# Weight slabs of a fused recurrent block, in halves through a ring of four

## What is computed

```python
h = rms_norm(x, norm_g)
xa, ga, q, f_pre, i_in, gb, gm = split(h @ w_in)          # w_in: 1024 x 8192
ya = rg_lru(causal_conv4(xa)) * silu(ga)                  # gated linear recurrence
o  = hgrn2_chunked(silu(q), 1 - f, i_in, log(f))          # 8 heads, state 128 x 128
yb = rms_norm(o) * silu(gb)
g_a, g_b = split(sigmoid(gm + b_merge))
x = x + (g_a * (ya @ proj_a) + g_b * (yb @ proj_b)) @ w_out
return rms_norm(x, final_norm_g)
```

## Time and profile before

| | us |
|---|---|
| median of the timed runs (2) | 1841.28 |
| lowest, highest | 1828.49, 1854.06 |
| the profiled execution | 1826.28 |
| its span, slowest core (core 1) | 1824.7 |
| spans of the 8 cores | 1814.4 to 1824.7 |

### The profile page before, as it was taken

The page is one execution under the profiler, slowest core; times in us unless marked ns, Lnnn a source line. Parts: engine busy times, 40 slices in busy tenths (PEclk is TensorE's granted clock), DMA queues, the critical chain, the costliest instruction groups (busy, mean ns, idle before and its releaser), DMA issues.

```text
span 1824.7 us, 24273 instructions; the slowest of 8 cores (1814.4 to 1824.7 us)
## 1 busy us (share of the span) xinstructions
PE 1497.1 (82%) x7552; PEld 706.6 (39%) x7552; DVE 1077.5 (59%) x1764; ACT 988.4 (54%) x2007; POOL 102.7 (6%) x118
## 2 busy tenths in 40 slices
PE   1786769998698977989689985989869997899866
PEld 0332244343443434434443434434344344443342
DVE  0543465575664676656655756656667467566664
ACT  3262472657537563574826666275744757256571
POOL 0000010000100001000000001000010000100010
PEclk9898879999799998999889997999979998899978
DMA  9999936632135412354035431353213631243302
GB/s 197 197 193 180 184 92 185 223 145 95 47 138 189 170 57 93 137 187 149 37 139 172 152 139 47 109 214 139 93 56 130 231 139 47 98 179 139 139 1 92
DMA packets 33404, 243.96 MB, mean 134 GB/s; under 512 B 2048, under 2 KB 2176, under 8 KB 22016
## 3 DMA queue, kind: packets, MB, share of 16 engines
q0 software_dynamic: 22816, 185.08, 33.5%
q1 hardware_dynamic: 10464, 57.33, 9.2%
HBM read 226.15 MB, written 39.85 MB: 146 GB/s over the span
## 4 chain that ended last, share of the span: by engine, by line
PE 63%; ACT 14%; DMA 9%; issue 8%; DVE 5%; DVEq 0%; ACTq 0%; POOL 0%; POOLq 0%; SPq 0%
PE PS L394 47%; PE PS L405 9%; DMA WS<-w_in 8%; ACT SQJ L655 2%; ACT R L545 2%; DVE R L500 2%; PE PS L680 2%; ACT Q L582 1%; DVE ATT L624 1%; ACT Q L580 1%; PE PS L602 1%; ACT Q L585 1%; PE PS L649 1%; DMA wbf<-WS 1%; ACT Q L487 1%
## 5 line engine op out<-in xcount | busy, mean ns | idle before, releaser
L394 PE MATMUL PS<-HT,WS 128*128 128x512 bf16 x3584 | 801.7, 386 | 70.3 <-DMA WS<-w_in 40.6
L394 PEld LDWEIGHTS PS<-HT,WS 128*128 128x128 bf16 x3584 | 352.7, 99 | 514.6 <-issue 113.9
L548 DVE TENSOR_TENSOR_SCAN R<-ONES,R 128x512 f32<-128x512 f32 x64 | 75.4, 1210 | 142.3 <-ACT R L545 142.3
L463 DVE SCALAR_TENSOR_TENSOR R<-R,PAR 128x512 f32<-128x512 f32 x192 | 144.3, 751 | 20.4 <-DVE R L463 0.5
L443 ACT ACTIVATE HT<-PS,PAR 128x512 bf16<-128x512 bf16 x64 | 37.9, 704 | 207.6 <-PE PS L441 207.6
L500 DVE SCALAR_TENSOR_TENSOR R<-R 128x512 f32<-128x512 f32 x64 | 39.9, 692 | 182.4 <-ACT R L497 182.1
L394 PE MATMUL PS<-R,WS 128*128 128x512 bf16 x512 | 128.3, 418 | 12.9 <-DVE R L683 12.9
L394 PE MATMUL PS<-Q,WS 128*128 128x512 bf16 x512 | 115.2, 384 | 22.6 <-DVE Q L553 13.0
L405 PE MATMUL PS<-WS,HT 128*128 128x512 bf16 x512 | 117.6, 389 | 17.2 <-DVE R L504 16.6
L649 PE MATMUL PS<-R 128*128 128x128 bf16 x256 | 66.2, 266 | 64.4 <-DVE ATT L624 62.4
L405 PE MATMUL PS<-WS,Q 128*128 128x512 bf16 x512 | 112.8, 379 | 0.0
(11 more groups left out here) (106 smaller groups left out, 2077.1 us busy)
## 6 DMA issues: line engine op xcount, KB each, us to landing
WS<-wbf POOLq DMA_DIRECT2D x77, 2048.0 KB, 8.1
wbf<-WS SPq DMA_DIRECT2D x11, 2048.0 KB, 13.7
XT<-x SPq DMA_DIRECT2D x8, 2048.0 KB, 13.8
WS<-w_in POOLq DMA_DIRECT2D x8, 2048.0 KB, 31.0
y<-XT SPq DMA_DIRECT2D x8, 2048.0 KB, 13.2
WS<-proj_a POOLq DMA_DIRECT2D x1, 2048.0 KB, 23.9
WS<-proj_b POOLq DMA_DIRECT2D x1, 2048.0 KB, 24.8
WS<-w_out POOLq DMA_DIRECT2D x1, 2048.0 KB, 15.4
```

The lines of the kernel that those rows point to most:

```text
L394: P.emit("pe", lambda e, W=W, ps=ps, k=k, m=m: e.matmul(ps[:, :], W[:, k, m * 128:(m + 1) * 128], src(k), start=(k == 0), stop=(k == 7)), ...
L463: P.emit("dve", lambda e, k=k: e.scalar_tensor_tensor(XC.ap(m), XA.ap(m, k, k + TT), par(P_CW + 8 * k + m), XC.ap(m), ALU.mult, ALU.add), ...
L548: P.emit("dve", lambda e: e.tensor_tensor_scan(BB.ap(hd), ONES[:, 0:1].to_broadcast([128, TT]), SS.ap(hd), 0.0, ALU.mult, ALU.add), reads= ...
```

## The change

Each slab is cut into two halves of 512 output columns, h = 0 and 1. `WS` becomes four buffers of 128 x 8 x 512 (the same SBUF in all), each with its own buffer record and its own load and store semaphores. `wbf` has 22 entries of 8 KB in each partition. `next_w(name, h)` hands out one half and issues loads until those of the three following halves (`PREF = NWS - 1`) are issued. In tile 0 a load reads runs of 512 float32 columns (2 KB) and writes runs of 1 KB; each load has its store. `proj_fm` takes a new half at m = 0 and m = 4. `proj_tm` now has the half outside and the row groups j inside, where before j was outside.

```diff
@@ -209,7 +209,7 @@
     dram["fng"] = nc.dram_tensor("fng", [128, D], F32, kind="ExternalInput").ap()
     dram["consts"] = nc.dram_tensor("consts", [128, 256], F32, kind="ExternalInput").ap()
     dram["y"] = nc.dram_tensor("y", [NB * SEQ, D], F32, kind="ExternalOutput").ap()
-    dram["wbf"] = nc.dram_tensor("wbf", [11, 128, 8 * D], BF16, kind="Internal").ap()
+    dram["wbf"] = nc.dram_tensor("wbf", [22, 128, 8 * 512], BF16, kind="Internal").ap()
     dbg = None
     if debug is not None:
         dbg = nc.dram_tensor("dbg", list(debug), F32, kind="ExternalOutput").ap()
@@ -249,7 +249,8 @@
         ONB = sb("ONB", [128, D], BF16)
         WX = sb("WXb", [128, 8, 128], BF16)
         WA = sb("WAb", [128, 8, 128], BF16)
-        WS = [sb("WS%d" % i, [128, 8, D], BF16) for i in range(2)]
+        NWS = 4
+        WS = [sb("WS%d" % i, [128, 8, 512], BF16) for i in range(NWS)]
         b_XT = [[Buf("XT%d_%d" % (i, j)) for j in range(4)] for i in range(2)]
         b_HT = [Buf("HT%d" % c) for c in range(NCH)]
         b_SQJ, b_PAR, b_DP, b_FNG = Buf("SQJ"), Buf("PAR"), Buf("DP"), Buf("FNG")
@@ -262,7 +263,7 @@
         b_ATT4 = [Buf("ATT4_%d" % i) for i in range(2)]
         b_ONB = Buf("ONB")
         b_WX, b_WA = Buf("WX"), Buf("WA")
-        b_WS = [Buf("WS0"), Buf("WS1")]
+        b_WS = [Buf("WS%d" % i) for i in range(4)]
 
         XW = 516
         R1 = Region(nc, es, "R1", 8 * XW * 4, gran=XW * 4)
@@ -315,7 +316,7 @@
         s_ld = [sem("ld_x0"), sem("ld_x1")]
         s_c = [sem("ld_c%d" % i) for i in range(5)]
         s_st = [sem("st_y0"), sem("st_y1")]
-        s_w = [sem("ld_w0"), sem("ld_w1")]
+        s_w = [sem("ld_w%d" % i) for i in range(4)]
         out_ops = []
 
         P.emit("sp", lambda e: e.dma_start(out=PAR[:, :], in_=dram["params"]), writes=[b_PAR], dma_sem=s_c[0])
@@ -352,20 +353,21 @@
             WORDER = ["xa", "ga", "gma", "pa", "f", "q", "gb", "i"]
         else:
             WORDER = ["xa", "ga", "gma", "i", "gb", "q", "f", "pa", "gmb", "pb", "wo"]
+        NHC = 2 * len(WORDER)
+        total_w = NB * NT * NHC
         wstate = {"n": 0, "issued": 0}
-        total_w = NB * NT * len(WORDER)
-
-        b_WBF = [Buf("WBF%d" % i) for i in range(len(WORDER))]
-        s_wst = [sem("st_w0"), sem("st_w1")]
+        b_WBF = [Buf("WBF%d" % i) for i in range(NHC)]
+        s_wst = [sem("st_w%d" % i) for i in range(NWS)]
+        PREF = NWS - 1
 
         def issue_w(idx):
             if idx >= total_w:
                 return
-            k = idx % len(WORDER)
-            name = WORDER[k]
-            s = idx % 2
-            if idx < len(WORDER):
-                src = WSRC[name].rearrange("(k p) n -> p k n", p=128)
+            k = idx % NHC
+            name, h = WORDER[k // 2], k % 2
+            s = idx % NWS
+            if idx < NHC:
+                src = WSRC[name][:, h * 512:(h + 1) * 512].rearrange("(k p) n -> p k n", p=128)
                 P.emit("pool", lambda e, s=s, src=src: e.dma_start(out=WS[s][:, :, :], in_=src),
                        writes=[b_WS[s]], dma_sem=s_w[s], name="ldw_" + name)
                 P.emit("sp", lambda e, s=s, k=k: e.dma_start(out=dram["wbf"][k], in_=WS[s][:, :, :].rearrange("p k n -> p (k n)")),
@@ -374,35 +376,37 @@
                 P.emit("pool", lambda e, s=s, k=k: e.dma_start(out=WS[s][:, :, :].rearrange("p k n -> p (k n)"), in_=dram["wbf"][k]),
                        reads=[b_WBF[k]], writes=[b_WS[s]], dma_sem=s_w[s], name="ldwb_" + name)
 
-        def next_w(name):
+        def next_w(name, h):
             idx = wstate["n"]
-            assert WORDER[idx % len(WORDER)] == name, (name, WORDER[idx % len(WORDER)])
-            if idx == 0:
-                issue_w(0)
-            issue_w(idx + 1)
+            assert WORDER[(idx % NHC) // 2] == name and idx % 2 == h, (name, h, idx)
+            while wstate["issued"] <= min(idx + PREF, total_w - 1):
+                issue_w(wstate["issued"])
+                wstate["issued"] += 1
             wstate["n"] = idx + 1
-            return WS[idx % 2], b_WS[idx % 2]
+            return WS[idx % NWS], b_WS[idx % NWS]
 
         def proj_fm(wname, src, src_bufs, consume, before=None):
-            W, bW = next_w(wname)
             for m in range(8):
+                if m % 4 == 0:
+                    W, bW = next_w(wname, m // 4)
                 if before is not None:
                     before(m)
                 P.lab = wname
                 ps, bps = next_ps()
+                mm = m % 4
                 for k in range(8):
-                    P.emit("pe", lambda e, W=W, ps=ps, k=k, m=m: e.matmul(ps[:, :], W[:, k, m * 128:(m + 1) * 128], src(k), start=(k == 0), stop=(k == 7)),
+                    P.emit("pe", lambda e, W=W, ps=ps, k=k, mm=mm: e.matmul(ps[:, :], W[:, k, mm * 128:(mm + 1) * 128], src(k), start=(k == 0), stop=(k == 7)),
                            reads=[bW] + src_bufs(k), writes=[bps])
                 consume(m, ps, bps)
 
         def proj_tm(wname, src, src_bufs, consume):
-            W, bW = next_w(wname)
-            P.lab = wname
-            for j in range(4):
-                for half in range(2):
+            for half in range(2):
+                W, bW = next_w(wname, half)
+                P.lab = wname
+                for j in range(4):
                     ps, bps = next_ps()
                     for k in range(8):
-                        P.emit("pe", lambda e, W=W, ps=ps, k=k, j=j, half=half: e.matmul(ps[:, :], src(k, j), W[:, k, half * 512:(half + 1) * 512], start=(k == 0), stop=(k == 7)),
+                        P.emit("pe", lambda e, W=W, ps=ps, k=k, j=j: e.matmul(ps[:, :], src(k, j), W[:, k, :], start=(k == 0), stop=(k == 7)),
                                reads=[bW] + src_bufs(k), writes=[bps])
                     consume(j, half, ps, bps)
 
```

## The result

The changed kernel takes 1849.02 us (median of 11 runs) beside 1830.69 us for the kernel before (median of 10). The ratio is 1.0096, 95% interval 1.0076 to 1.0117: about 18 us slower, inside the 2% that was called no change, and on the other side of the 5 us of gain that were forecast. The median before that the prediction started from, 1841.28, came from two runs; over more it is 1830.69, near the profiled execution.

A forecast was written before the change was run, and what follows sets the result against it. Tile 0's full DMA stretch before gmb was taken as the bound; -5 - 6 + 6 + 0 = -5 us gave 1821 from the profiled execution, 1836 from the median. Forecast 1832, between them, called no change; range 1806 to 1866.

The forecast's parts named there:

- What bounds the kernel: Full DMA stretch before gmb of tile 0, a row of weight loads; later tiles keep 215.1 us and can't gain.
- Half a slab less: Ahead of gmb in tile 0: its first half needs 8.5 slabs loaded, not 9; gain 5 us, bounds 0 and 7.3.
- tails: Tile 0 loads: the queue empties before each landing, three halves in flight fill it; gain 6 us, bounds 0 and 8.
- Shorter rows: Tile 0 loads: 2 KB runs double the packets, with 23 ns each independent of size; +6 us, bounds 0 and +132.
- The Trainium skill on run length: Tile 0 loads: line rate from 512 B up, so the short-run term would be 0 and the time 6 us lower.
- Twice as many transfers: All weight transfers: some 2.5 us fixed per transfer lie beside other transfers; cost 0, without that cover +43 us.
- Rival C: Tile 0 transfers: the per-transfer part isn't hidden, half of 43 us shows; +10 us, 1842 us, chance 0.08.
- POOL, order of the loops, the added wait: More POOL reload issues, proj_tm's exchanged loops and PE's wait in mid-slab: each cost 0; bounds 42 us for POOL, 2 for order.
- The base: Time before the change: profiled execution 1826.28 us, median of two timed runs 1841.28; forecast 1832 lay between 1821 and 1836.
- B: Tile 0 stream gets quicker through finer mixing, 208 GB/s for 191; 23 us faster, 1814 us, chance 0.16.
- D: The ring does nothing, transfer time in tile 0 is moved, not saved; 0 to -2 us, 1836 us, chance 0.12.
- A: Tile 0 loads: a 2 KB run costs 0.65 of a 4 KB one (149 ns); +29 us, 1861 us, chance 0.22.

The follow-up runs named there:

- The run with neighbouring runs: Changed kernel, but in tile 0 eight loads take both halves of a slab row by row, as neighbouring 2 KB runs; 0.995 of the kernel before, 1819.09 us.
- the control with two slabs and eight loads: Kernel before, with each slab loaded in tile 0 by eight DMAs of 128 whole rows, runs of 4 KB; 0.9959 of the kernel before.
- The run with two ahead: Changed kernel with two halves issued ahead instead of three (PREF = NWS - 2), nothing else changed; 1.01 of the kernel before.
- the run cut by rows: Kernel before with its two slabs, each slab cut by k into two DMAs for load, store and reload, runs of 4 KB; 0.9969, 1822.29 us.

## Why the prediction was wrong, point by point

- *What bounds the kernel.* Right. The period of the later tiles moved by 0.3 us, PE never waits for a reload, and the difference is there before `gmb` of tile 0. Putting off bytes moved tile 0: 29 us in `pb` for eight stores (38 were expected for `gmb`), and 8 us in the whole for one x tile (5 to 6 expected).
- *Half a slab less, and tails: -5 and -6.* Neither term was measured by itself. In the changed kernel the first half of `gmb` came 13 us later than before and not 7 sooner, under the dearer loads. The run with neighbouring runs gains 9 us, near the 11 forecast, but that is luck: in tile 0 it has neither the half-slab lead nor the single slots, and the control with two slabs and eight loads gains as much without a ring (0.9959). The run with two ahead equals that with three within its interval. That the ring gives these 11 us isn't shown.
- *Shorter rows: +6 us.* This step failed. It took the cost of a short packet as a fixed part of the packet, 23 ns from the earlier trace rows, and let half of it hide behind a shared limit, since `wo`'s load shows 146 ns for a long packet alone. What was measured is 144 to 146 ns for half a row, 30 ns over the 115 of its bytes, and none of it hidden: 32 us between the two directions of the cut, 27 us between the changed kernel and the one with neighbouring runs. The fixed part itself wasn't wrong. The median packet takes 98 ns for 1 KB and 173 ns for 2 KB on every core of the kernels above, and 2 x 98 - 173 = 23. What differs is the dear packets. Of those of 1 KB, one in ten takes over 276 ns in the changed kernel and over 120 in the one with neighbouring runs (slowest cores, 0 to 215 us). With neighbouring runs these rarer long ones make up for most of the 23 ns in the mean (120 ns beside 117), with the column cut they add to it. The sum -5 - 6 + 32 would have been +21 us; the measured difference is 18.
- *The Trainium skill on run length.* In DMA: Bandwidth & Descriptors, section Specifications, 512 B is enough for line rate. As far as size goes the neighbouring runs nearly agree (1 KB written, 2 KB read, 120 ns beside 117 for half of a whole row). The same length spread out does not: 147.6 ns. The rule says nothing of the place, and by it alone the change would have been forecast 6 us quicker and been further off.
- *Twice as many transfers: 0.* Right: 0.9969 with two, 0.9959 with eight for each slab. Rival C has fallen. But the 384 GB/s of the earlier trace rows that it started from is not a reload: by the queues of that stretch all but one of its packets are the store of `wo`. The runs give the fixed part better. A reload of 2,048 KB lands in 8.1 us and one of 1,024 KB in 5.1, so the second half of the bytes takes 3.0 us and some 2.1 us belong to the transfer (an estimate).
- *POOL, order of the loops, the added wait: 0.* Right as far as tested: 1.0006 for the order; the run cut by rows has the 77 more reload instructions and the wait in the middle of a slab too, and is quicker than before.
- *The base.* 1832 is the forecast with its 5 us of gain, so no change stood at 1837. Rivals B and D count from 1837, A and C from 1832: by its own terms A's price was 1866 and C's 1847. The median before is now 1830.69, so even no change would have come out 6 us under that base.
- *The rivals.* A came true by its place, its price per packet (149 ns, measured 146) and its condition (from 124 ns); its 29 us of loss were 18. It had the right number for a partly wrong reason: it was the length of the run there, and in the runs the same length costs 4 ns where its neighbour is read beside it. B had 16% and is excluded in the changed kernel (176 GB/s for 191), though not by its reason: with neighbouring runs the stream does reach 196 to 209 GB/s.

## What to carry to other kernels

When a load is cut into pieces for a finer pipeline, look at what it does to the order of the addresses and not only at the length of a run: cut a matrix so that each piece is still read in whole rows (by k here), or have the pieces of a row read one behind the other. Between the cut by columns and the cut by rows lay 32 us of this kernel, while landing in pieces gained 6 to 14 us in the runs that read whole or neighbouring rows; a stretch with the DMA engines at 0.98 had nothing to hide such a cost behind. And in such a stretch count bytes first: 2.1 MB that nobody needed yet were worth as much as any finer pipeline of two or eight pieces that reads whole rows.

## What the runs showed that wasn't expected

With all eight cores reading float32 weights at once, a run of 2 KB took 142 to 149 ns in the changed kernel and 119 to 123 ns in the two kernels that read its neighbour beside it (packets of 1 KB written, means of each core, 0 to 215 us). For a load with nothing else on its core's queues the difference is small. The last half of `wo` in the changed kernel has a row pitch of 4 KB and nothing beside it; DMA from 286 to 301 us, GB/s in 40 slices of 0.375 us:

```profile
GB/s 0 0 22 0 0 0 0 0 0 0 0 0 0 0 0 0 0 0 0 0 0 33 49 126 120 188 191 205 210 202 199 202 205 210 213 199 194 38 11 0
```

About 204 GB/s in the middle, 16 x 1,024 B / 204 GB/s = 80 ns for each packet, where the long runs of the earlier trace rows go at some 215, 76 ns for half a row.

Is it the crowd or the pitch? No run separates the two, but the packets can be counted off in the order in which they start, 2,048 to a matrix. Means over the eight cores, in the changed kernel and in the one with neighbouring runs: the seven matrices of w_in from xa to f (pitch 32 KB) 139 to 156 ns beside 116 to 128, and gmb 145 beside 122; pa, which lies between f and gmb with a pitch of 4 KB, 133 beside 126; pb 126 beside 116 and wo 110 beside 111. So the matrices of w_in pay 16 to 36 ns for the column cut, pa in the same crowd 7, and pb behind it 10. This speaks for the pitch as the larger part, and against the number of transfers, which changed for pa as well. It is a count and not an experiment. What in the memory it is, no run here tells.
